# In a filler's slot the weights are split one chunk ahead of the filler's own, not two

## The chip, the cores and the metric

The kernel runs on one core of one Trainium2 chip. The metric is the device time of one execution in microseconds; the median of three runs of the kernel before is 2589.95 us (2587.48 to 2590.49). TensorE (PE) multiplies matrices into PSUM, VectorE (DVE) and ScalarE (ACT) do the elementwise work, and SyncE (SP) issues the transfers of the weights.

## The reference, cut to what matters

Two transformer stacks of two layers each run one after the other on a sequence of 256 tokens with 1024 features, all in float32:

```python
for l in range(DEPTH):                                  # first_block, DEPTH = 2
    h = rms_norm(x, norm_mix[l])
    x = x + (even_mixer if l % 2 == 0 else odd_mixer)(h, ...)   # projections, two kinds of attention, w_out
    x = x + memory_cross_attention(rms_norm(x, norm_cross[l]), rms_norm(mem, norm_mem[l]), ...)
    x = x + conv_ffn(rms_norm(x, norm_ffn[l]), ...)
for l in range(DEPTH):                                  # second_block
    x = x + HALF_STEP * swiglu(rms_norm_2(x, ffn1_norm[l]), ...)
    x = x + hybrid_mixer(rms_norm_2(x, mix_norm[l]), ...)       # fox, sparse and stick-breaking attention, gates
    x = x + memory_cross_attention_2(rms_norm_2(x, ca_norm[l]), rms_norm_2(mem, mem_norm[l]), ...)
    x = x + HALF_STEP * swiglu(rms_norm_2(x, ffn2_norm[l]), ...)
return rms_norm_2(x, final_norm)
```

Every `@` with a weight matrix is a linear layer. There are 8 mixers and cross attentions, and 6 feed-forward layers.

## The kernel before, in words

**Weights.** A weight matrix is cut into *chunks* of at most 128 x 2048 float32 (1 MB), numbered through the whole program in the order of use. Each chunk takes four steps. SP loads it into one of 3 slots `raw` (L639). ACT rounds it to `whi` (L1140), in one of 3 sets. DVE subtracts, `wlo = raw - whi` (L1503). PE multiplies with it, three products for each block: hi by lo, lo by hi, hi by hi (L727, L728, L730). ACT and DVE together *split* a chunk. ACT may not overwrite a set until PE has finished with the chunk three before (the `release` of the chunk). SP may not reload a slot until DVE has split the chunk three before (L635).

**Units.** A *unit* is one bank of PSUM: all products of (mostly) 256 output columns, 48 matmuls with a full chunk, 24 in an output projection, where two units share a chunk. Two banks alternate, so a unit waits until the unit two before has been *evacuated*, by ACT or by DVE, to SBUF.

**Stages.** The program is a list of stages, and PE, ACT and DVE each walk through it with a loop of their own. A `linear` stage works on its own units. For unit `un`, ACT and DVE first call `split_upto(un["chunk"] + 2)` and then evacuate. `heads`, `attention` (softmax, mlstm, difference, stick) and `index` stages compute attention, where PE would often wait, so units of the *next* linear layers are put between as *fillers*. A stage has a table `fill={slot: (emit_end, evac_end)}`: at that slot PE emits the units below `emit_end`, ACT and DVE split ahead and then evacuate the units below `evac_end`. The slot `"pre"` comes right behind the barrier at a stage's start (PE does it before its barrier), slots 0, 1, ... are turns of the attention loop or places in `heads`. A filler table advances by one unit a slot nearly everywhere.

**Where it is.** `split_upto` of ACT stands at L1124 to L1140, of DVE at L1489 to L1503, `fill` of ACT at L1160 and of DVE at L1545. In an attention loop on DVE the order of a turn is `fill`, then the softmax work of the units; on ACT `fill`, then the exponentials. In a `linear` stage whose output is a residual, DVE adds unit i to x (L1532), ACT then prepares two tiles of the next layer's input (L1186, L1189: `norm_pair`), and the next layer's first products (L757) start from those.

Filled stages in the order of time: the even mixer (heads, softmax, mlstm, heads, then a linear), the odd mixer (heads, softmax, heads, difference, heads, then a linear), four cross attentions (two with a heads stage, each ending in a linear of two chunks and four units), and two hybrid mixers (heads, index, three attentions, then the linear over three branches, whose chunks have 1536 and 768 columns in turn).

Of the kernel before, what the change touches and what calls it, by code (L numbers as in the profile page):

```python
# [159 lines left out]
def build(nc, io):  # L160
    ctx = ExitStack()
    with ctx:
# [104 lines left out]
        stages, chunks, units_of = [], [], []  # L267
# [836 lines left out]
        def _(eng):  # L1104
# [10 lines left out]
            def enter(i, st):  # L1115
                if i and not st["join"]:
                    eng.drain().then_inc(S["act_stage"], 1)
                    eng.wait_ge(S["pe_stage"], st["bar"])
                    eng.wait_ge(S["dve_stage"], st["bar"])
                    fill(st, "pre")  # L1120
# [3 lines left out]
            def split_upto(c):  # L1124

                while rounded[0] <= min(c, len(chunks) - 1):
                    i = rounded[0]
                    rounded[0] += 1
                    ch = chunks[i]
                    eng.wait_ge(loaded[i % SLOTS], ch["loaded"])  # L1130
                    if ch["mem"] is not None:
                        eng.wait_ge(S["lin_ready"], ch["last"] + 1)
                        eng.activation(X[ch["mem"]][0][:, :, :], raw[i % SLOTS][:, :].rearrange("p (k c) -> p k c", c=SEQ), ACT.Copy)\
                           .then_inc(S["weights_hi"], 1)
                        continue
                    s = ch["set"]
                    if s >= SETS:
                        name, value = chunks[set_chunks[s - SETS]]["release"]
                        eng.wait_ge(S[name], value)
                    eng.activation(whi[s % SETS][:, 0:ch["n"]], raw[i % SLOTS][:, 0:ch["n"]], ACT.Copy).then_inc(S["weights_hi"], 1)  # L1140
# [3 lines left out]
            def evac_upto(end):  # L1144

                while moved[0] < end:
                    u = moved[0]
                    un = units_of[u]
                    moved[0] += 1
                    if un["post"] != "plain":  # L1150
                        continue
                    eng.wait_ge(S["lin_ready"], u + 1)
                    if "dsts" in un:
                        (a, b, dst, _), = un["dsts"]
                        src = lin_bank[u % 2][:, :].rearrange("p (t c) -> p t c", t=QT)[:, :, a:b]
                    else:
                        dst, src = un["dst"], lin_bank[u % 2][:, 0:un["n"] * SEQ].rearrange("p (n c) -> p n c", c=SEQ)
                    eng.activation(dst, src, ACT.Copy).then_inc(S["lin_moved"], 1)

            def fill(st, slot):  # L1160

                if slot in st["fill"]:
                    emit_end, evac_end = st["fill"][slot]
                    split_upto(units_of[emit_end - 1]["chunk"] + 2)
                    evac_upto(evac_end)

            gated = [0]
# [118 lines left out]
            def heads(st):  # L1286
                if st["d"]:
                    norms_of_heads(st)
                    fill(st, 0)
                    fill(st, 1)  # L1290
                if st["gates"]:
                    gate_logs(st["gates"])
                for i, g in enumerate(st["groups"] if st["rope"] else ()):
                    eng.wait_ge(S["qk_roped"], st["r0"] + i + 1)
                    eng.activation(g["x"], banks[(3, 7)[i % 2]][:, 0:g["n"] * SEQ].rearrange("p (n c) -> p n c", c=SEQ), ACT.Copy).then_inc(S["qk_rot_used"], 1)
                    if i == 1 and not st["d"]:
                        fill(st, 0)

                if st["gates"]:
                    gate_rows(st["gates"])  # L1300
# [167 lines left out]
        def _(eng):  # L1468
# [9 lines left out]
            def enter(i, st):  # L1478
                if i and not st["join"]:
                    eng.drain().then_inc(S["dve_stage"], 1)  # L1480
                    eng.wait_ge(S["pe_stage"], st["bar"])
                    eng.wait_ge(S["act_stage"], st["bar"])
                    fill(st, "pre")
                if i == more_consts_at:
                    eng.wait_ge(S["more_consts_loaded"], 16)
# [3 lines left out]
            def split_upto(c):  # L1489

                while subtracted[0] <= min(c, len(chunks) - 1):
                    i = subtracted[0]
                    subtracted[0] += 1
                    ch = chunks[i]
                    n, full = ch["n"], raw[i % SLOTS]
                    eng.wait_ge(S["weights_hi"], i + 1)
                    if ch["mem"] is not None:
                        hi, lo = X[ch["mem"]]
                        eng.tensor_tensor(lo[:, :, :], full[:, :].rearrange("p (k c) -> p k c", c=SEQ), hi[:, :, :].bitcast(F32), ALU.subtract)\
                           .then_inc(S["weights_split"], 1)  # L1500
                        continue
                    s = ch["set"] % SETS
                    eng.tensor_tensor(wlo[s][:, 0:n], full[:, 0:n], whi[s][:, 0:n].bitcast(F32), ALU.subtract).then_inc(S["weights_split"], 1)  # L1503
# [3 lines left out]
            def evac_upto(end):  # L1507
                while evacuated[0] < end:
                    evacuated[0] += 1
                    evac(evacuated[0] - 1)  # L1510
# [34 lines left out]
            def fill(st, slot):  # L1545

                if slot in st["fill"]:
                    emit_end, evac_end = st["fill"][slot]
                    split_upto(units_of[emit_end - 1]["chunk"] + 2)
                    evac_upto(evac_end)  # L1550

            def norm_lo(nm, p):
# [145 lines left out]
            def heads(st):  # L1698
# [3 lines left out]
                if st["d"]:  # L1702
                    R = st["rows"]
                    eng.wait_ge(S["qk_rs"], st["n"] + 1)
                    newton(rstd[0:R, 0, 0:SEQ], rstd2[0:R, 0, 0:SEQ], post_bank[0][0:R, 0:SEQ], st["d"] * EPS, 0.5, S["qk_rows"], C(st["scale"])[0:R, :])
                    fill(st, 0)
                    for i, g in enumerate(gs):
                        eng.wait_ge(S["qk_spread"], g0 + i + 1)
                        norms = banks[i % 4][:, 0:g["n"] * SEQ].rearrange("p (n c) -> p n c", c=SEQ)
                        eng.scalar_tensor_tensor(out=g["x"], in0=g["x"], scalar=cols[:, g["gain"]:g["gain"] + 1], in1=norms,  # L1710
                                                 op0=ALU.mult, op1=ALU.mult).then_inc(S["qk_normed"], 1)
                    fill(st, 1)
# [311 lines left out]
```

## Time and profile before

| | |
|---|---|
| median of three runs | 2589.95 us |
| the profiled execution: its own time | 2590.67 us |
| its span | 2588.8 us |
| PE busy | 2394.8 us (93%) |
| DVE busy | 1603.0 us (62%) |
| ACT busy | 1096.6 us (42%) |
| chain of waits, by engine | PE 77%, DVE 11%, ACT 6% |
| granted TensorE clock, mean | 0.952 |
| a 1 MB load of weights, median from issue to landing | 5.1 us |

The span is what the trace covers; 1.9 us of the execution lie outside it. Shares of busy time are averages over the whole program; in the feed-forward layers PE never stops, in the filled stages it waits here and there, and only there can the order of the splits matter.

### The profile page before, as it was taken

The page shows a single profiled execution, that of the slowest core. Times are in us where ns is not written, and L with a number is a line of the kernel's source. Part 1 is how long each engine was busy: PE and PEld are TensorE (multiplying, and loading weights), DVE is VectorE, ACT ScalarE, POOL GpSimd, SP SyncE. Part 2 cuts the span into 40 slices and gives each one's busy share as a digit, 9 for nine tenths or more (in the row PEclk, how much of TensorE's full clock was granted, in tenths as well). Part 3 has the DMA queues.
Part 4 walks back from the last instruction along what each step waited for, and adds up shares of the span by engine and source line. Part 5 has one row for each costly group of instructions (what it writes and reads, how often), then busy time and mean ns, then how long its engine had stood idle before and what let it go on. Part 6 is the DMA issues. An engine that isn't in the chain of part 4 may idle for free.

```text
span 2588.8 us, 41000 instructions
## 1 busy us (share of the span) xinstructions
PE 2394.8 (93%) x17744; PEld 2239.1 (86%) x17744; DVE 1603.0 (62%) x2326; ACT 1096.6 (42%) x1329; POOL 34.8 (1%) x60
## 2 busy tenths in 40 slices
PE   6989999998799999999998799999999988889997
PEld 5868899986689999999967688999999967688997
DVE  4565587755457786656557646666666446655654
ACT  4435454533444444335334345334334324445332
POOL 1300000000000000000000000000000000000000
PEclk8889999998799999999989899999999989899999
DMA  8523245441134555555521344555556522244552
GB/s 256 173 70 132 96 165 194 164 146 59 56 129 167 187 172 179 186 176 153 180 78 54 113 163 136 176 177 182 177 179 179 172 66 77 68 151 145 175 185 82
DMA packets 318901, 373.79 MB, mean 144 GB/s; under 512 B 23647, under 2 KB 289651, under 8 KB 317571
## 3 DMA queue, kind: packets, MB, share of 16 engines
q1 hardware_dynamic: 313715, 353.32, 41.7%
q0 software_dynamic: 3424, 11.50, 1.5%
q10 hardware_dynamic: 1584, 6.36, 0.7%
q8 instruction: 140, 2.29, 0.4%
q14 instruction: 38, 0.31, 0.0%
HBM read 361.97 MB, written 9.18 MB: 143 GB/s over the span
## 4 chain that ended last, share of the span: by engine, by line
PE 77%; DVE 11%; ACT 6%; issue 2%; PEld 2%; DMA 1%; DVEq 0%; PEldq 0%; ACTq 0%
PE bank L727 20%; PE bank L730 20%; PE bank L728 20%; DVE wlo L1503 3%; ACT whi L1140 3%; PE bank L757 2%; PE bank L758 2%; PE bank L737 2%; PE bank L968 2%; PE bank L1017 2%; PE bank L761 2%; PE bank L897 1%; PE bank L1004 1%; ACT x_hi L1186 1%; DVE xT L1532 1%
## 5 line engine op out<-in xcount | busy, mean ns | idle before, releaser
L727 PE MATMUL bank<-x_hi,wlo 128*128 128x256 f32 (+1 forms) x4432 | 1143.9, 290 | 24.3 <-DVE wlo L1503 8.3
L728 PE MATMUL bank<-x_lo,whi 128*128 128x256 f32 (+1 forms) x4432 | 1131.4, 287 | 0.0
L1503 DVE TENSOR_TENSOR wlo<-raw,whi 128x2048 fp32r<-128x2048 f32 (+2 forms) x344 | 762.0, 2224 | 324.4 <-ACT whi L1140 324.2
L1140 ACT ACTIVATE whi<-raw 128x2048 fp32r<-128x2048 f32 (+2 forms) x344 | 638.9, 1860 | 719.4 <-PE bank L730 651.5
L727 PEld LDWEIGHTS bank<-x_hi,wlo 128*128 128x128 f32 (+1 forms) x4432 | 869.5, 196 | 51.5 <-issue 31.5
L728 PEld LDWEIGHTS bank<-x_lo,whi 128*128 128x128 f32 (+1 forms) x4432 | 870.2, 196 | 0.0
L730 PE MATMUL bank<-x_hi,whi 128*128 128x256 f32 x4432 | 710.9, 286 | 0.0
L730 PEld LDWEIGHTS bank<-x_hi,whi 128*128 128x128 f32 x4432 | 615.7, 195 | 4.6 <-issue 0.7
L757 PE MATMUL bank<-x_hi,wlo 128*128 128x256 f32 x544 | 154.8, 315 | 46.5 <-DVE xT L1532 19.8
L757 PEld LDWEIGHTS bank<-x_hi,wlo 128*128 128x128 f32 x544 | 111.3, 205 | 52.2 <-issue 32.0
L758 PE MATMUL bank<-x_lo,whi 128*128 128x256 f32 x544 | 144.1, 295 | 0.0
L1938 DVE TENSOR_TENSOR wk<-bank,norm_scale 128x512 f32<-128x512 f32 x132 | 91.1, 690 | 83.5 <-PE bank L730 77.4
L758 PEld LDWEIGHTS bank<-x_lo,whi 128*128 128x128 f32 x544 | 111.5, 205 | 1.2
L1976 DVE CAST x_hi<-wk 128x512 fp32r<-128x512 f32 x66 | 28.2, 427 | 131.9 <-PE bank L730 130.9
L1954 DVE SCALAR_TENSOR_TENSOR wk<-wk,cols 128x255 f32<-128x255 f32 x176 | 73.5, 480 | 48.0 <-ACT wk L1434 47.3
L727 PE MATMUL bank<-whi,x_lo 128*128 128x256 f32 (+2 forms) x400 | 99.7, 286 | 1.1 <-issue 0.8
L728 PE MATMUL bank<-wlo,x_hi 128*128 128x256 f32 (+2 forms) x400 | 98.5, 283 | 0.0
L1186 ACT ACTIVATE x_hi<-xT,con,cols 128x256 fp32r<-128x256 f32 x112 | 60.8, 590 | 84.7 <-DVE xT L1532 69.9
L1434 ACT ACTIVATE wk<-wk,cols 128x256 f32<-128x256 f32 x88 | 45.7, 590 | 98.1 <-DVE wk L1938 98.1
L1017 PE MATMUL bank<-wk,vt 128*64 128x256 f32 (+2 forms) x288 | 72.9, 392 | 11.4 <-ACT wk L1389 9.8
L727 PEld LDWEIGHTS bank<-whi,x_lo 128*128 128x128 f32 x400 | 77.7, 194 | 4.3 <-issue 3.8
L968 PE MATMUL bank<-ft 64*128 64x128 f32 (+2 forms) x216 | 62.8, 431 | 19.1 <-DVEq L1480 17.1
(225 smaller groups left out, 1986.9 us busy)
## 6 DMA issues: line engine op xcount, KB each, us to landing
raw<-in_ffn_w_gu SPq DMA_DIRECT2D x88, 1024.0 KB, 5.1
raw<-in_ffn_w_down SPq DMA_DIRECT2D x66, 1024.0 KB, 5.2
raw<-in_ffn_w_up SPq DMA_DIRECT2D x44, 1024.0 KB, 5.1
raw<-in_w_in SPq DMA_DIRECT2D x42, 1024.0 KB, 5.2
raw<-in_ca_w_kv SPq DMA_DIRECT2D x16, 1024.0 KB, 5.1
raw<-in_od_w_in SPq DMA_DIRECT2D x12, 1024.0 KB, 5.1
raw<-in_ev_w_in SPq DMA_DIRECT2D x10, 1024.0 KB, 5.3
raw<-in_w_in SPq DMA_DIRECT2D x20, 512.0 KB, 5.2
```

The lines of the kernel that those rows point to most:

```text
L727: eng.matmul(out, a[1], b[0], start=first and i == 0, stop=False, skip_group_check=True)
L728: eng.matmul(out, a[0], b[1], start=False, stop=False, skip_group_check=True)
L730: m = eng.matmul(out, a[0], b[0], start=False, stop=last and i == len(operands) - 1, skip_group_check=True)
L757: eng.matmul(bank[:, o], a[1], b[0], start=i == 0 and k == 0, stop=False, skip_group_check=True)
L758: eng.matmul(bank[:, o], a[0], b[1], start=False, stop=False, skip_group_check=True)
L968: m = eng.matmul(o, un["q"][:, t * P:(t + 1) * P], un["k"][:, 0:n], start=True, stop=row is None)
L1017: m = eng.matmul(ob[i % len(ob)][un["pb"]:un["pb"] + un["d"], q0:SEQ], un["v"][:, k, :], probsT_flat[i % 2][:, at:at + SEQ - q0], start=k ...
L1140: eng.activation(whi[s % SETS][:, 0:ch["n"]], raw[i % SLOTS][:, 0:ch["n"]], ACT.Copy).then_inc(S["weights_hi"], 1)
L1186: eng.activation(X[nm["buf"]][0][:, k, :], xT[:, k, :], ACT.Identity, scale=cols[:, nm["gain"] + k:nm["gain"] + k + 1], bias=C("zero")).th ...
L1503: eng.tensor_tensor(wlo[s][:, 0:n], full[:, 0:n], whi[s][:, 0:n].bitcast(F32), ALU.subtract).then_inc(S["weights_split"], 1)
L1938: return eng.tensor_tensor(wk[:, half, :].rearrange("p (n c) -> p n c", c=SEQ), bank[:, :].rearrange("p (n c) -> p n c", c=SEQ), norms, AL ...
L1954: m = eng.scalar_tensor_tensor(out=o, in0=wk[:, half, i * SEQ:(i + 1) * SEQ][:, src], scalar=cols[:, w:w + 1], in1=o, op0=ALU.mult, op1=AL ...
```

## The change

In a filler's slot ACT and DVE split up to one chunk ahead of the last unit emitted there, where they split up to two ahead before. `linear` and `ffn` stages still split two ahead.

```diff
@@ fill, ScalarE (L1160) and, the same line, VectorE (L1545)
                 if slot in st["fill"]:
                     emit_end, evac_end = st["fill"][slot]
-                    split_upto(units_of[emit_end - 1]["chunk"] + 2)
+                    split_upto(units_of[emit_end - 1]["chunk"] + 1)
                     evac_upto(evac_end)
```

All splits are still done, each once and in the same sequence; what moves is where they stand among the other instructions. On ScalarE in the even mixer's mlstm stage (L1357 and L1360 are its exponentials; the numbers name the sets and slots):

```order
-L1140 ACTIVATE whi1<-raw1 128x2048 [waits weights_loaded1,lin_ready,dve_stage,pe_stage]
+L1140 ACTIVATE whi0<-raw0 128x2048 [waits weights_loaded0,lin_ready,dve_stage,pe_stage]
 L1357 ACTIVATE wk<-wk,stat 128x256 [waits att_max]
 L1357 ACTIVATE wk<-wk,stat 128x256 x3
 L1360 ACTIVATE stat<-stat 128x4
-L1140 ACTIVATE whi2<-raw2 128x2048 [waits lin_ready,weights_loaded2]
+L1140 ACTIVATE whi1<-raw1 128x2048 [waits lin_ready,weights_loaded1]
 L1357 ACTIVATE wk<-wk,stat 128x256 [waits att_max]
 L1357 ACTIVATE wk<-wk,stat 128x256 x3
```

The place has a split before and after, but of the chunk before the former one, so `lin_ready` is waited for at an earlier value.

On VectorE at the end of the first cross attention (L1858 and L1860 are the last attention output, L1532 the residual of the linear stage's units):

```order
 L1858 CAST x0_hi<-bank7 128x256 [waits att_o]
 L1860 TENSOR_TENSOR x0_lo<-bank7,x0_hi 128x256 [waits dve_step]
-L1503 TENSOR_TENSOR wlo0<-raw1,whi0 128x2048 [waits weights_hi,act_stage,pe_stage]
+L1503 TENSOR_TENSOR wlo2<-raw0,whi2 128x2048 [waits weights_hi,act_stage,pe_stage]
+L1503 TENSOR_TENSOR wlo0<-raw1,whi0 128x2048 [waits weights_hi]
 L1532 TENSOR_TENSOR xT<-bank4,xT 128x512 [waits lin_ready]
 L1532 TENSOR_TENSOR xT<-bank5,xT 128x512 [waits lin_ready]
```

The linear stage behind the filled ones now opens with two splits where it had one; ScalarE's order moves in the same way. The split that is missing is the one of the first `"pre"` slot of each run of filled stages.

On VectorE in the first hybrid mixer's stick stage (three pieces in order of time: its first slot, its second, and the start of the linear stage behind it, whose first residual-like step is L1538):

```order
-L1503 TENSOR_TENSOR wlo2<-raw1,whi2 128x1536
+L1503 TENSOR_TENSOR wlo1<-raw0,whi1 128x2048
 L1528 SCALAR_TENSOR_TENSOR gt<-bank5,norm_scale 128x512
 L1777 SCALAR_TENSOR_TENSOR ft<-bank0,ft 128x384
...
-L1503 TENSOR_TENSOR wlo0<-raw2,whi0 128x768
+L1503 TENSOR_TENSOR wlo2<-raw1,whi2 128x1536
 L1528 SCALAR_TENSOR_TENSOR gt<-bank4,norm_scale 128x512
...
+L1503 TENSOR_TENSOR wlo0<-raw2,whi0 128x768
 L1503 TENSOR_TENSOR wlo1<-raw0,whi1 128x1536
 L1538 SCALAR_TENSOR_TENSOR ft<-gt,bank4 128x512
```

Here the chunks have unequal sizes, so the slots get larger splits than before. PE, SP and POOL keep their order word for word.

## Rows read from the trace of the kernel before

**Rows 1.** The page's chain that ended last, shares of the span:
```profile
PE 77%; DVE 11%; ACT 6%; issue 2%; PEld 2%; DMA 1%; DVEq 0%; PEldq 0%; ACTq 0%
```
**Rows 2.** The page's groups: line, operation, count, busy us, mean ns, idle before:
```profile
L1503 DVE TENSOR_TENSOR wlo<-raw,whi 128x2048 fp32r<-128x2048 f32 (+2 forms) x344 | 762.0, 2224 | 324.4 <-ACT whi L1140 324.2
L1140 ACT ACTIVATE whi<-raw 128x2048 fp32r<-128x2048 f32 (+2 forms) x344 | 638.9, 1860 | 719.4 <-PE bank L730 651.5
```
**Rows 3.** Timeline, ScalarE, mlstm: start us, length us, instruction, idle before and releaser:
```profile
157.99 0.19 ACT L1360 ACTIVATE stat<-stat 128x4 f32<-128x4 f32 x1
161.29 1.91 ACT L1140 ACTIVATE whi<-raw 128x2048 fp32r<-128x2048 f32 x1 [3.12 <-PE bank L730]
```
**Rows 4.** Timeline, VectorE, the same slot of the mlstm stage:
```profile
163.23 2.29 DVE L1503 TENSOR_TENSOR wlo<-raw,whi 128x2048 fp32r<-128x2048 f32 x1 [6.89 <-ACT whi L1140]
```
**Rows 5.** Timeline, TensorE, behind the filler of that slot:
```profile
169.73 0.80 PE L955 MATMUL bank<-ft 128*128 128x256 f32 x1 [3.54 <-DVE wk L1846]
```
**Rows 6.** Timeline, ScalarE, the linear stage that ends the first cross attention:
```profile
286.94 1.91 ACT L1140 ACTIVATE whi<-raw 128x2048 fp32r<-128x2048 f32 x1 [2.23 <-DVEq L1480]
291.91 1.09 ACT L1186 ACTIVATE x_hi<-xT,con,cols 128x256 fp32r<-128x256 f32 x2 [3.06 <-DVE xT L1532]
...
293.72 1.10 ACT L1186 ACTIVATE x_hi<-xT,con,cols 128x256 fp32r<-128x256 f32 x2 [0.19 <-DVE xT L1532]
...
295.24 1.90 ACT L1140 ACTIVATE whi<-raw 128x2048 fp32r<-128x2048 f32 x1
```
**Rows 7.** Timeline, VectorE, the same linear stage:
```profile
288.98 2.29 DVE L1503 TENSOR_TENSOR wlo<-raw,whi 128x2048 fp32r<-128x2048 f32 x1 [2.17 <-ACT whi L1140]
291.19 0.68 DVE L1532 TENSOR_TENSOR xT<-bank,xT 128x512 f32<-128x512 f32 x1
292.99 0.69 DVE L1532 TENSOR_TENSOR xT<-bank,xT 128x512 f32<-128x512 f32 x1 [1.11 <-PE bank L730]
...
297.18 2.29 DVE L1503 TENSOR_TENSOR wlo<-raw,whi 128x2048 fp32r<-128x2048 f32 x1 [2.71 <-ACT whi L1140]
299.39 0.68 DVE L1532 TENSOR_TENSOR xT<-bank,xT 128x512 f32<-128x512 f32 x1
```
**Rows 8.** Timeline, TensorE, the first product of the feed-forward layer behind it:
```profile
300.22 0.35 PE L757 MATMUL bank<-x_hi,wlo 128*128 128x256 f32 x1 [1.51 <-DVE xT L1532]
```
**Rows 9.** Timeline, VectorE, the even mixer's linear stage:
```profile
210.97 2.29 DVE L1503 TENSOR_TENSOR wlo<-raw,whi 128x2048 fp32r<-128x2048 f32 x1 [0.94 <-ACT whi L1140]
215.56 0.69 DVE L1532 TENSOR_TENSOR xT<-bank,xT 128x512 f32<-128x512 f32 x1 [2.30 <-PE bank L761]
```
**Rows 10.** Timeline, ScalarE, first slot of the first stick stage:
```profile
1409.98 1.49 ACT L1140 ACTIVATE whi<-raw 128x1536 fp32r<-128x1536 f32 x1
```
**Rows 11.** Timeline, VectorE, first and second slot of that stick stage:
```profile
1411.60 1.76 DVE L1503 TENSOR_TENSOR wlo<-raw,whi 128x1536 fp32r<-128x1536 f32 x1 [3.04 <-ACT whi L1140]
...
1421.49 0.95 DVE L1503 TENSOR_TENSOR wlo<-raw,whi 128x768 fp32r<-128x768 f32 x1
```
**Rows 12.** Timeline, TensorE, the scores of that stage's third head:
```profile
1417.30 0.92 PE L976 MATMUL bank<-ft 64*128 64x128 f32 x4 [0.87 <-DVE wk L1790]
```
**Rows 13.** Timeline, VectorE, the first hybrid mixer's linear over three branches:
```profile
1445.88 1.76 DVE L1503 TENSOR_TENSOR wlo<-raw,whi 128x1536 fp32r<-128x1536 f32 x1 [5.11 <-ACT whi L1140]
1447.67 0.69 DVE L1538 SCALAR_TENSOR_TENSOR ft<-gt,bank 128x512 f32<-128x512 f32 x1
```
**Rows 14.** Timeline, TensorE, the third unit of that linear stage:
```profile
1448.51 0.35 PE L727 MATMUL bank<-x_hi,wlo 64*128 64x256 f32 x1 [2.29 <-DVE ft L1538]
```
**Rows 15.** Timeline, ScalarE, behind the "pre" split of the first cross attention:
```profile
254.56 2.17 ACT L1307 ACTIVATE wk<-ft 128x512 f32<-128x512 f32 x4
```
**Rows 16.** Timeline, TensorE, the sums over those squares, behind the "pre" filler:
```profile
258.03 2.33 PE L884 MATMUL bank<-wk,con 128*8 128x256 f32 x10
```
**Rows 17.** Windows: us, busy of PE, PEld, DVE, ACT, POOL, then clock, DMA:
```profile
1448.80:1455.60 6.80, 6.80 (x27) 5.77 (x26) 3.50 (x6) 1.48 (x1) 0.00 (x0) 0.50 0.54 154
...
300.00:307.00 7.00, 6.78 (x50) 6.60 (x51) 5.16 (x9) 6.21 (x8) 0.00 (x0) 1.00 0.48 152
```

More of the change, by code:

```diff
@@ L1548, in fill @@
                     emit_end, evac_end = st["fill"][slot]
-                    split_upto(units_of[emit_end - 1]["chunk"] + 2)
+                    split_upto(units_of[emit_end - 1]["chunk"] + 1)
                     evac_upto(evac_end)
```

## The prediction

> **What bounds the kernel now.** I read the chain of waits first. It lies on PE for 77% of the span, on DVE for 11% and on ACT for 6% [rows 1]. The feed-forward layers are PE's alone and keep their order; DVE and ACT are on the chain in the mixers and cross attentions, and those are the stages that the change touches. Then the groups: 344 splits of 1.86 us on ACT and 2.22 us on DVE, in which DVE mostly waits for ACT and ACT mostly for PE to give a set free [rows 2]. The reader should not add this up: most of it is feed-forward, where it costs nothing. So I went through the timeline, one filled stage after another, with three questions: does PE wait here, what ends the wait, and does a split stand ahead of that.
>
> **The change as a whole.** No split is added or removed. A run of filled stages loses the split of its first "pre" slot (8 places: the first heads stage of each mixer and of two cross attentions, the attention of the other two) and its closing linear stage gets one more at its start (8 places). Between them every slot keeps one split, of the chunk before. That has two effects: ACT waits for an earlier release, and where chunks are unequal the slot's length changes.
>
> **The 8 opening splits, removed: 0.** In the first cross attention ACT, behind the split, squares the heads' inputs until 256.7 [rows 15], and PE takes up the squares at 258.03, with no idle time before, because its own filler ends only then [rows 16]. The cover is the "pre" filler, which ends 1.3 us later than the squares; taking 1.91 us away from ACT only widens that. Where I looked at the other openings, PE ran through in the same way. I take 0. The bound above is 0, the bound below 8 times 1.91 us off.
>
> **The release in the mlstm stage: 3.1 us saved.** ACT finishes its exponentials at 158.18 and then sits until 161.29, because the split in the second slot needs the set of a chunk on which PE is still busy with the filler of the slot before [rows 3]. DVE waits 6.89 us for it, splits from 163.23 [rows 4], and only then scales the probabilities for which PE waits 3.54 us [rows 5]. After the change the same place splits a chunk whose set has long been free. ACT starts at 158.15 or so, DVE at 160.1, ends at 162.3, behind the filler's end at 161.2 that its evacuation needs. Everything behind follows 3.1 us earlier, as DVE and ACT alternate on the chain until the stage ends. Late next is PE, whose next filler ends at 169.73 - 3.54 = 166.2, against probabilities at 169.7 - 3.1 = 166.6: there is hardly more to be had. Bounds: nothing saved, and 3.5 us, PE's wait. Elsewhere such waits for a release are under a filler of PE and give nothing.
>
> **The closing linear stages of the four cross attentions: 2.0 us lost each, 8.1 in all.** Now ACT splits once [rows 6], DVE behind it from 288.98, and adds unit 0 right behind that split, at 291.19, without waiting for PE [rows 7]. With two splits ACT does the second from 288.85, beside DVE's first. DVE does its two back to back, starts 2.21 us apart as between these rows, so unit 0 is added at 288.98 + 2 x 2.21 = 293.40. Unit 1, ready on PE since about 292.9, follows at once. ACT prepares the next layer's tiles 0.72 us behind unit 0's addition (291.91 - 291.19), so from 294.12; the second pair 1.62 us later without idle time (293.72 - 291.91 - 0.19), from 295.74; its next split 1.52 us after (295.24 - 293.72), at 297.26 instead of 295.24. Behind this split stand DVE's split and the addition of unit 2 [rows 7], for which the feed-forward's first product waits [rows 8]. That is 2.0 us later at the start of the feed-forward layer, and nothing behind gives it back. The timeline has the same rows at 760, 1565 and 2361 us. Bounds: 0, if the wait of 1.51 us and the others took it up, and 4.2 us, both halves of a split end to end.
>
> **The closing linear stages of the even and odd mixer: 0.** DVE splits at 210.97 and next has to add a unit that PE has ready only at 215.56 [rows 9]. A second split ends at 210.97 + 2.21 + 2.29 = 215.47, just in time; the odd mixer's linear stage has the same shape. The cover is PE's pair of units. If it fails, 0.1 us or so.
>
> **The hybrid mixers: 1.8 us lost each, 3.5 in all.** The stick stage's first slot now holds a split of 2048 columns instead of 1536. On ACT that is 1.91 - 1.49 = 0.42 us more [rows 10], on DVE 2.29 - 1.76 = 0.53 [rows 11], and both stand one behind the other on the way to the scores of the third head, for which PE waits on DVE [rows 12]. So 0.95 us; a filler stands behind those scores and the next head behind the filler, so it stays. The second slot grows from 768 to 1536 columns, 1.76 - 0.95 = 0.8 us on DVE [rows 11]; a filler of PE lies beside it, and I take 0, between 0 and 0.8. In the linear stage behind, ACT does a 768 split ahead of the 1536 one, about 0.8 us, DVE's 0.95 us of it lies beside ACT's second, and the first merge moves from 1447.67 to 1448.45 [rows 13]; PE waits for just that merge [rows 14]. So 0.8. Bounds for a whole mixer: 0, and 3.5 us, every added piece of ACT and DVE end to end.
>
> **Transfers: 0.** A slot is reloaded when its chunk is split, so reloads move by one slot in the filled stages. The latest is the second chunk of the feed-forward layer: its reload can now start only when the first of the two closing splits ends, at 291.3, and it is needed behind the feed-forward's first product, after 302. A megabyte takes 5.1 us from issue to landing (the page's DMA part), so another one ahead of it fits too.
>
> **Sum.** -3.1 + 8.1 + 1.9 + 1.6 = 8.5 us. The profiled execution took 2590.67 us, so 2599.2; it stands 0.72 us above the median, which gives 2598.4 us as the median after. The bounds taken all together run from 3.5 us faster to 4 x 4.2 + 2 x 3.5 = 24 us slower, without the openings. Below 0.2%, 5.2 us, a measurement of this kernel can't tell a change from none.
>
> **Rivals.**
>
> 1. *PE's clock falls on top.* In the cross attentions' closing stages PE's waits grow: one of about 1.1 us arises before unit 2 (unit 0 added by 294.1, PE free from 292.9), and the 1.51 us become about 2.1. In the hybrid's linear a wait of 2.29 us [rows 14] is followed by 6.8 us at a granted clock of 0.50, 1.2 GHz [rows 17], while behind the 1.51 us it stays at 1.00, 2.4 GHz [rows 17]. One such stretch costs 3.4 us of PE's work. If two of the four get one, the sum is 15.3 and the time 2605. Against it: the added waits are shorter than 2.29 us. The Trainium skill, "TensorE: Matmul & The Clock Gate", section "What's actually happening", says that the default is the slow clock and that activity releases it, so more waiting can only hurt; the rows agree in direction, and by that rule this rival would be the forecast.
>
> 2. *The cross attentions hide the second split.* Then -3.1 + 3.5 = 0.4 and the time is 2590.4: no change. For it: PE waits 1.51 us before the feed-forward layer anyway. Against it: that wait ends by the very addition that moves.
>
> 3. *Faster: the opening splits were on the path.* If the squares behind the "pre" split, and not the filler, held PE's sums, each of the 8 openings would give 1.91 us, 15.3 in all, and 8.5 - 15.3 = -6.8 puts the time at 2583. It decides from the point where a "pre" filler ends before ACT's squares do. Against it are the 1.3 us of room [rows 15, 16].
>
> 4. *The change doesn't do what it says*, as PE would at some slot stand before a chunk that is not split yet. Each filler's chunk is still split in the slot before its own, and DVE passes that slot before PE gets to the next. Where it did happen, it would cost up to 4.2 us a time; I count it with rival 1.
>
> **How the numbers follow.** The forecast has 0.57, with a range of its own of 2595 to 2602. Rival 1 (with 4) has 0.15, rival 2 with its partial forms, in which the terms shrink below 5.2 us, 0.21, rival 3 0.07. So slower 0.72, the same 0.21, faster 0.07. The range of 2592 to 2606 takes in rival 1 and half of rival 2's and leaves out rival 3.
>
> **What would show it.** Right: ACT's L1140 in the mlstm stage starts at about 158.1 with no wait for PE, and PE's wait of 3.54 us is gone; the four cross attentions' linear stages show two L1503 in a row and the first L1532 2.2 us later, the feed-forward's first product 2.0 us later; the mixers' additions at 215.56 don't move against the product's start; the third stick head's scores start 0.95 us later; openings on PE look as before. Wrong: PE's L757 behind the cross attentions starts as far from the stage's start as now; a heads stage gets shorter; PE waits for L1503 inside a filled stage; or the stretches at half clock add up to more than the terms.

## The result, and the profile after

| | before | changed |
|---|---|---|
| median, four runs each | 2588.72 us | 2603.6 us |
| the profiled execution: time, span | 2590.67, 2588.8 us | 2604.47, 2602.6 us |
| chain of waits | PE 77%, DVE 11%, ACT 6% | PE 76%, DVE 12%, ACT 7% |
| granted TensorE clock, mean | 0.952 | 0.952 |

The changed kernel is slower: the ratio is 1.0062, 95% interval 1.0049 to 1.0075, 13 to 19 us. The forecast of 2598.4 us had the sign and its range (2592 to 2606) holds the time, but it gives only a bit more than half of the loss.

TensorE runs the same instructions in the same order in both kernels, so I followed the start of each of them through both traces. Where the difference of the starts jumps, time is lost or won. I call this comparison the ledger. These are its jumps from before to after, in us:

| stretch | forecast | trace |
|---|---|---|
| start to the mlstm stage (not the change's, see below) | 0 | -3.5 |
| mlstm stage | -3.1 | -3.2 |
| closing stages of the four cross attentions, to the feed-forward's first product | 4 x 2.0 = 8.1 | 1.90, 1.91, 2.18, 1.91 = 7.9 |
| the feed-forward layers' first part behind them | 0 | 1.46, 1.58, 1.59, 1.59 = 6.2 |
| first hybrid mixer, second | 1.75 each | 3.4, 3.1 |
| the rest: other openings, the other mixers' closings | 0 | about 0 |

The sum is 13.8 us but for rounding, the difference of the spans. First the mlstm stage, which answers to [rows 3 to 5]: timeline of the changed kernel, start us, length us, instruction, idle before and releaser.

```profile
154.47 0.19 ACT L1360 ACTIVATE stat<-stat 128x4 f32<-128x4 f32 x1
154.56 1.90 ACT L1140 ACTIVATE whi<-raw 128x2048 fp32r<-128x2048 f32 x1
156.49 2.29 DVE L1503 TENSOR_TENSOR wlo<-raw,whi 128x2048 fp32r<-128x2048 f32 x1 [3.67 <-ACT whi L1140]
162.98 1.13 PE L955 MATMUL bank<-ft 128*128 128x256 f32 x4 [1.84 <-DVE wk L1846]
```

ScalarE's split starts right behind the exponentials, its wait of 3.12 us is gone, and VectorE's wait has fallen from 6.89 to 3.67 us. TensorE still waits 1.84 us, where it waited 3.54. From ScalarE's last exponential (L1360) to the product L955 it is 8.51 us here, 11.74 before [rows 3, 5].

Not all of that is the change's. The release that ScalarE waited for comes from TensorE's filler, and in the trace of before this filler ran at half clock. The kernel `e10_hybrid_heads_slot` below has these splits as before, but its filler ran at full clock. First its ScalarE, then the windows over the filler, before and in that kernel:

```profile
154.90 0.19 ACT L1360 ACTIVATE stat<-stat 128x4 f32<-128x4 f32 x1
155.19 1.91 ACT L1140 ACTIVATE whi<-raw 128x2048 fp32r<-128x2048 f32 x1
```

```profile
152.00:158.60 6.60, 6.60 (x30) 6.07 (x29) 4.17 (x12) 1.80 (x5) 0.00 (x0) 0.50 0.46 151
```

```profile
149.00:155.50 6.50, 6.50 (x52) 6.37 (x52) 4.15 (x12) 2.12 (x6) 0.00 (x0) 1.00 0.49 155
```

Its split starts 0.10 us behind the exponentials without the change, and from L1360 to L955 it is 8.72 us. So the change is worth 3.2 us here when the filler runs at half clock, and 0.2 when it does not. Of the five traces with these splits as before, three have the whole wait (3.11 or 3.12 us), one has 1.60 and one none.

The closing stage of the first cross attention answers to [rows 6 to 8]. It starts at 280.20 here, at 286.94 before.

```profile
280.20 3.72 ACT L1140 ACTIVATE whi<-raw 128x2048 fp32r<-128x2048 f32 x2 [2.23 <-DVEq L1480]
282.25 4.49 DVE L1503 TENSOR_TENSOR wlo<-raw,whi 128x2048 fp32r<-128x2048 f32 x2 [2.18 <-ACT whi L1140]
286.66 1.28 DVE L1532 TENSOR_TENSOR xT<-bank,xT 128x512 f32<-128x512 f32 x2
287.49 0.36 PE L727 MATMUL bank<-x_hi,wlo 128*128 128x256 f32 x1 [1.29 <-DVE xT L1532]
290.41 1.90 ACT L1140 ACTIVATE whi<-raw 128x2048 fp32r<-128x2048 f32 x1
292.34 2.29 DVE L1503 TENSOR_TENSOR wlo<-raw,whi 128x2048 fp32r<-128x2048 f32 x1 [3.34 <-ACT whi L1140]
294.55 0.68 DVE L1532 TENSOR_TENSOR xT<-bank,xT 128x512 f32<-128x512 f32 x1
295.38 0.36 PE L757 MATMUL bank<-x_hi,wlo 128*128 128x256 f32 x1 [1.90 <-DVE xT L1532]
```

Two splits in a row stand ahead of the first addition, which comes 6.46 us behind the stage's start instead of 4.25. TensorE now waits twice, 1.29 us before unit 2 and 1.90 before the feed-forward layer. From the stage's start to the layer's first product it is 15.16 us (295.38 - 280.22), against 13.26 (300.22 - 286.96).

Then the clock. Here are windows of 3.4 us at the feed-forward layers behind the second, third and fourth cross attention: columns as in [rows 17], the seventh is the granted clock. Before:

```profile
773.20:776.60 3.40, 3.39 (x25) 3.29 (x26) 2.87 (x7) 3.40 (x7) 0.00 (x0) 1.00 0.86 279
1578.70:1582.10 3.40, 3.39 (x25) 3.29 (x26) 2.87 (x7) 3.40 (x7) 0.00 (x0) 1.00 0.87 283
2374.20:2377.60 3.40, 3.40 (x27) 3.29 (x27) 2.79 (x7) 3.40 (x7) 0.00 (x0) 1.00 0.92 304
```

After:

```profile
773.10:776.50 3.40, 3.40 (x14) 3.04 (x14) 1.68 (x4) 3.40 (x5) 0.00 (x0) 0.50 1.08 387
1585.40:1588.80 3.40, 3.40 (x15) 3.04 (x14) 1.95 (x5) 3.40 (x5) 0.00 (x0) 0.51 0.83 284
2387.60:2391.00 3.40, 3.40 (x15) 3.04 (x14) 1.60 (x4) 3.40 (x5) 0.00 (x0) 0.50 0.70 245
```

TensorE is busy all through both, and gets through 25 to 27 instructions in one and 14 or 15 in the other. These are three new stretches at 1.2 GHz, 1.6 us each in the ledger. The mean clock doesn't show them, because other stretches went.

The 1.46 us at the first feed-forward layer are something else. TensorE does wait inside the first two feed-forward layers, for VectorE's splits. Its wait 43 us behind the first closing stage, before and after:

```profile
343.19 0.39 PE L727 MATMUL bank<-x_hi,wlo 128*128 128x256 f32 x1 [1.22 <-DVE wlo L1503]
338.33 0.39 PE L727 MATMUL bank<-x_hi,wlo 128*128 128x256 f32 x1 [2.70 <-DVE wlo L1503]
```

Before, a stretch of 3.4 us at half clock lay ahead of this wait and was taken up by it; after, the stretch lies behind it and costs its 1.5 us.

The first stick stage and the linear stage behind it [rows 10 to 14], after:

```profile
1412.11 2.29 DVE L1503 TENSOR_TENSOR wlo<-raw,whi 128x2048 fp32r<-128x2048 f32 x1 [3.46 <-ACT whi L1140]
1418.34 1.22 PE L976 MATMUL bank<-ft 64*128 64x128 f32 x3 [1.83 <-DVE wk L1790]
...
1449.49 0.96 DVE L1503 TENSOR_TENSOR wlo<-raw,whi 128x768 fp32r<-128x768 f32 x1 [4.46 <-ACT whi L1140]
1450.77 1.76 DVE L1503 TENSOR_TENSOR wlo<-raw,whi 128x1536 fp32r<-128x1536 f32 x1 [0.32 <-ACT whi L1140]
1452.56 0.69 DVE L1538 SCALAR_TENSOR_TENSOR ft<-gt,bank 128x512 f32<-128x512 f32 x1
```

TensorE's wait for the third head's scores grew from 0.87 to 1.83 us, the 0.95 of the forecast. What the forecast didn't have follows at once, in windows at the same place before and after:

```profile
1417.20:1424.00 6.80, 6.70 (x52) 6.32 (x52) 5.68 (x11) 3.49 (x7) 0.00 (x0) 1.00 0.04 15
```

```profile
1418.20:1425.00 6.80, 6.66 (x28) 6.01 (x29) 6.61 (x11) 3.35 (x6) 0.00 (x0) 0.50 0.05 16
```

### The profile page after: what moved, and what is told of

Its sections match the earlier page's. It is cut to its first block, busy times and chain, and to the rows that moved or that the text cites. A ratio compares the mean times of both kernels' runs of the same rounds, so it can differ in the third digit from the quotient of the medians.

```text
span 2602.6 us, 41000 instructions
## 1 busy us (share of the span) xinstructions
PE 2401.4 (92%) x17744; PEld 2244.2 (86%) x17744; DVE 1603.4 (62%) x2326; ACT 1096.0 (42%) x1329; POOL 34.9 (1%) x60
## 3 DMA queue, kind: packets, MB, share of 16 engines
q8 instruction: 140, 2.29, 0.4%
## 4 chain that ended last, share of the span: by engine, by line
PE 76%; DVE 12%; ACT 7%; issue 2%; PEld 2%; DMA 0%; DVEq 0%; ACTq 0%; PEldq 0%
PE bank L727 20%; PE bank L730 19%; PE bank L728 19%; DVE wlo L1503 4%; ACT whi L1140 3%; PE bank L757 3%; PE bank L758 2%; PE bank L737 2%; PE bank L968 2%; PE bank L1017 2%; PE bank L761 2%; PE bank L897 1%; ACT x_hi L1186 1%; PE bank L1004 1%; DVE wk L1756 1%
```

## The experiments

Theory: the chain terms of the forecast, and on top of them rival 1, new stretches at half clock behind waits that have grown. Rivals: the chain alone; and an accident of one execution. Times are ratios to the kernel before, run beside it on the same chip, with their 95% intervals; 0.001 is 2.6 us. The changed kernel was timed beside runs of before of its own, so a distance to it is the difference of two ratios, good to 4 or 5 us.

**One part of the change at a time.** `ahead=1` was given to some stages, the rest kept 2.

```diff
-                    split_upto(units_of[emit_end - 1]["chunk"] + 2)
+                    split_upto(units_of[emit_end - 1]["chunk"] + st.get("ahead", 2))
```

*The four cross attentions.* 

> One chunk ahead only in the filled stages of the four cross attentions, so that each closing linear stage starts with two splits. Theory of the chain: 2.0 us each, 8 us slower. Theory of the chain and the clock (rival 1 of the prediction): the same 8 us and about 1.6 us more at the start of each feed-forward layer, from stretches of 3.4 us at half clock that follow the longer waits: 14 us slower, with the stretches at 773, 1585 and 2388 us as in the changed kernel. If the stretches come from something else in the changed kernel (the hybrids, the mlstm stage, the accident of one execution), they are missing here and the time is 8 us above.

Measured: 1.0059 (1.0045 to 1.0073), 15 us. Even the lower end, 11.6 us, lies above the 8 us of the chain alone. The ledger has the same four closing terms (1.89, 1.91, 2.18, 1.91) and 1.59 at the second and third feed-forward layer. The fourth shows nothing (0.01), so the stretch isn't certain even where the waits are. This trace is of the slowest of the five executions (2606.18 us, median 2601.62), and 3.7 us of its ledger lie behind 2080 us at places that the edit doesn't touch. The two stretches and the chain come to 11.1 us, so the time can't tell one stretch more or less.

*The two hybrid mixers.* 

> One chunk ahead only in the filled stages of the two hybrid mixers. The forecast has 0.95 + 0.8 us for each, 3.5 us slower. If the longer waits of the stick stage also bring half-clock stretches, as in the trace of the changed kernel (a stretch of 6.8 us at 1418 that before lacks), it is 3.1 to 3.4 us each, 6 to 7 us slower. In the trace the first merge of the linear stage over three branches comes 0.8 us later against that stage's start.

Measured: 1.0032 (1.0014 to 1.0051), 4 to 13 us. The interval is wide because of one execution of ten at 2615.91 us; the medians lie 6.4 us apart. The ledger has 6.0 us in all and repeats the changed kernel's jump in the first stick stage (3.9 us in both), with a stretch of 6.8 us at 1418. The four closing stages are unchanged (0.00 each). But the first feed-forward layer is 1.50 us later here, though nothing before it was changed: of the 1.46 us in the table above, nothing can be put down to the change. That leaves the three stretches, 4.8 us.

*The mlstm stage.* 

> One chunk ahead only in the mlstm stage, two everywhere else. If the release wait is worth what the forecast says, 3.1 us faster than before; by the two traces, which lose 1.7 us from the stage's second slot to the heads behind it, 1.7 us faster. If that loss was the clock's, and not the split's, no change. In its trace ScalarE's split of the second slot starts right behind the exponentials without a wait for PE, and TensorE's wait of 3.54 us there is down to about 1.8. At the start of the feed-forward layers there is no new stretch at half clock, and the closing stages of the cross attentions are as before.

Measured: 0.9993 (0.9984 to 1.0002), no difference that can be told; 4.1 us faster is still inside. The ledger has -3.9 us in the stage, and +2.2 in the heads stage behind it. There the pre slot, which splits two ahead, now has two splits to do:

```profile
191.29 3.71 ACT L1140 ACTIVATE whi<-raw 128x2048 fp32r<-128x2048 f32 x2 [0.25 <-DVEq L1480]
193.33 4.49 DVE L1503 TENSOR_TENSOR wlo<-raw,whi 128x2048 fp32r<-128x2048 f32 x2 [2.34 <-ACT whi L1140]
195.45 1.89 PE L884 MATMUL bank<-wk,con 128*4 128x256 f32 x8 [1.56 <-ACT wk L1307]
198.57 0.36 PE L727 MATMUL bank<-x_hi,wlo 128*128 128x256 f32 x1 [1.24 <-DVE xT L1532]
```

TensorE waits 1.56 us for squares that stand behind the second split. That is rival 3's mechanism, and it takes two splits in an opening to bring it out. In the changed kernel the heads stage has one, and pays nothing.

**Where the split stands against the addition.** The changed kernel with, in VectorE's `linear`, the addition ahead of the split, at first in all stages with a residual:

```diff
-                    split_upto(un["chunk"] + 2)
+                    late = un["post"] in ("residual",)
+                    split_upto(un["chunk"] + (0 if late else 2))
...
                     evac_upto(un["u"] + 1)
+                    split_upto(un["chunk"] + 2)
```

> The changed kernel, and in the linear stages whose output is a residual VectorE adds the unit first and does the split of two chunks ahead behind it. If the loss of the cross attentions is the place of the split ahead of the addition, TensorE no longer waits 1.3 us before unit 2 nor 1.9 us before the feed-forward's first product: 3.2 us less in each of four, and 1.57 us less in each of the even and odd mixers, 16 us off the changed kernel, 1 us faster than before; with the half-clock stretches gone as well 22 us off, 7 us faster than before. If ScalarE's order or the transfers hold these stages, nothing changes against the changed kernel: 15 us slower than before.

Measured: 1.0031 (1.0020 to 1.0042), 8 us below the changed kernel, not 16 or 22. The closing stages gained 3.1 to 3.4 us each, as the theory has it, but the even and odd mixers lost 2.9 and 5.7 us. Two things go wrong there. The edit puts off the split of the next chunk too, which there is not done yet, and TensorE waits 1.55 us for it; this is made up by the next layer's first product. Then TensorE waits about 3.1 us for the addition of unit 3, which now stands behind a split, and this stays; in the odd mixer a stretch at half clock behind it adds 2.7 us. The second try keeps the next chunk's split ahead (`+ 1` instead of `+ 0`) and leaves the mixers alone:

> The changed kernel; in the closing linear stages of the cross attentions VectorE does only the split of the next chunk ahead of an addition, and that of two chunks ahead behind it. The mixers' closing stages are left alone, which the earlier run of this kind did not do. If the loss of the cross attentions is the place of that split, TensorE's waits of 1.28 and 1.90 us go, and with them the half-clock stretches: 3.2 + 1.6 us in each of four, 19 us off the changed kernel, 4 us faster than before. If the stretches stay, 13 us off, 2 us slower than before. If ScalarE or a transfer holds the stage, no change against the changed kernel, 15 us slower than before.

Measured: 1.0013 (1.0004 to 1.0022), 12.7 us off the changed kernel. The ledger gives 3.6, 3.6, 3.8 and 3.6 us in the closing stages and 0.4, 2.0, 0.3 and 0.6 behind them; no stretch at half clock is left there, but TensorE waits 0.84 us for the split that now comes last. So the place of the split ahead of the addition is shown as the cause of the cross attentions' loss. The time alone sits at "stretches stay", 13 us.

**The clock by itself.** Dummy matmuls of constants fill TensorE's two waits of each closing stage and change nothing else.

```diff
+                    keep = nm is None and parts is None and len(units) == 4
+                    for _ in range(8 if keep and i == 2 else 0):
+                        eng.matmul(banks[2][:, 0:P], C("add128"), C("ident"), start=True, stop=True)
                     if i >= 2 or (nm is None and parts is None):
                         unit(u)
+                    for _ in range(13 if keep and i == 3 else 0):
+                        eng.matmul(banks[2][:, 0:P], C("add128"), C("ident"), start=True, stop=True)
```

> The changed kernel with dummy matmuls on TensorE (of constants, into a bank that nothing reads) in its two waits of each cross attention's closing linear stage: 8 ahead of unit 2 and 13 behind unit 3, about 0.13 us each. They leave the chain alone and only keep TensorE busy. If the waits bring the half-clock stretch at the start of the feed-forward layers, the stretches go and the time is 4 to 6 us below the changed kernel, 9 to 11 us above before. If the stretches have another cause, they stay, and the time is that of the changed kernel, 15 us above before, or more where the dummies are longer than the waits.

Measured: 1.0068 (1.0056 to 1.0081), no gain. The dummies took 1.95 and 3.07 us, longer than the waits, which cost 1.0 us a stage. All three stretches went, and with them 1.6 us each; the dummies eat 3.9 us of that, and stretches elsewhere take the rest. With 5 and 8 of them:

> The changed kernel with dummy matmuls in TensorE's two waits of each closing stage as before, but 5 and 8 of them instead of 8 and 13, since one takes 0.24 us and the earlier ones were longer than the waits by 0.7 and 1.2 us. If the half-clock stretches at the start of the feed-forward layers come from these waits, and nothing else is changed by the dummies, 4.8 to 6.2 us faster than the changed kernel, 9 to 10 us slower than before. If the stretches come of their own, 15 us slower than before.

The timeline of TensorE in this kernel, where each dummy shows as two records, and the first of the windows above:

```profile
760.79 1.28 PE L872 MATMUL bank<-con 128*128 128x128 f32 x10
762.24 0.36 PE L727 MATMUL bank<-x_hi,wlo 128*128 128x256 f32 x1 [0.17 <-DVE xT L1537]
768.06 1.95 PE L876 MATMUL bank<-con 128*128 128x128 f32 x16
```

```profile
770.10:773.50 3.40, 3.38 (x25) 3.29 (x26) 2.87 (x7) 3.40 (x7) 0.00 (x0) 1.00 0.86 287
```

In the trace this is clear: the four closing terms are unchanged (0.00, 0.00, 0.01, 0.00), the three stretches are gone, and the layers' starts are 1.6 us faster each. One trace could be an accident, but every kernel's trace has the four places. Three kernels have both waits and leave them unfilled: the changed one, the one with the cross attentions alone and the one with two ahead in the pre slots, below. They have a stretch that starts within 1.5 us of the layer's first product in 8 of 12 places (3, 2 and 3 of 4). The other eleven kernels, the two with dummies among them, have it in none of 44. That TensorE's idle time in the two waits brings the stretches is thereby shown in the traces.

The times don't bear it out: 1.0058 (1.0045 to 1.0070), 15 us above before where 9 to 10 were expected. The profiled execution (2599.12 us) was the fastest of five; the others reach 2604.45. Even the profiled one loses 1.6 us near 2067 us and 1.7 behind 2500, in half-clock stretches that are longer or new there though nothing was changed. Where TensorE's clock falls differs from one execution to the next, and whether the others lost the whole gain again in such places stays open.

**The openings.** The changed kernel with two ahead in the pre slots:

```diff
-                    split_upto(units_of[emit_end - 1]["chunk"] + 1)
+                    split_upto(units_of[emit_end - 1]["chunk"] + (2 if slot == "pre" else 1))
```

> The changed kernel, except that the first slot of a stage (pre) splits two ahead as before; slots 0, 1, ... split one ahead. So the eight openings have their split back, in the cross attentions and wherever else the pre slot is followed by slots without a new chunk. If the openings cost nothing, the time is that of the changed kernel, 15 us above before. If the missing opening splits were worth something (rival 3), it is up to 15 us slower than the changed kernel; and if the openings' place is what the closing stages need, it would be faster than the changed kernel.

Measured: 0.9997 (0.9988 to 1.0005), none of the three: 17 us faster than the changed kernel. The closing stages are as slow as before (0.00 against the changed kernel), and the openings show nothing. The time comes from a place that the prediction doesn't look at, the rotations in the hybrid mixers' heads stage (L1725 and L1726 on VectorE, L909 and L910 on TensorE), -7.9 us in the first and -9.2 in the second against before; 1.5 of the latter are a shorter stretch at half clock ahead of it. With a split in the opening, slot 0 of that stage has none. The kernel before:

```profile
1290.20 1.90 ACT L1140 ACTIVATE whi<-raw 128x2048 fp32r<-128x2048 f32 x1
1292.14 2.29 DVE L1503 TENSOR_TENSOR wlo<-raw,whi 128x2048 fp32r<-128x2048 f32 x1 [11.51 <-ACT whi L1140]
1294.35 0.68 DVE L1528 SCALAR_TENSOR_TENSOR gt<-bank,norm_scale 128x512 f32<-128x512 f32 x1
1294.95 0.68 DVE L1725 TENSOR_TENSOR wk<-ft,con 128x512 f32<-128x512 f32 x1
1296.29 2.08 PE L909 MATMUL bank<-wk,con 128*128 128x512 f32 x2 [6.40 <-DVE wk L1726]
```

VectorE waits for ScalarE's split, does its own and an evacuation, and only then prepares the next rotation (L1725, L1726), for which TensorE waits 6.40 us; then it runs at half clock, with L909 at 2.08 us. This stood in the trace of before, and the change leaves it as it is, since it swaps one chunk for another in that slot. So I tried it alone, in the kernel before: `ahead=1` for that heads stage, with pre slots at 2, which moves this split to the next stage's start.

> Two chunks ahead as in before, but in slot 0 of the hybrid mixers' heads stage one ahead, which leaves that slot without a split (its chunk comes two at a time in the index stage's pre slot). The run with two ahead in the pre slots alone was 15 us faster than forecast, and its trace lost 7.9 and 9.2 us in just these two stages. If this one split is the cause, 16 us faster than before, with ScalarE's and VectorE's steps of the rotations 4.8 us earlier behind the third and the rest from half-clock stretches that go. If it was the accident of one execution, no change.

Measured: 0.9945 (0.9933 to 0.9958), 14 us faster than before. The same rotation:

```profile
1285.39 0.69 DVE L1725 TENSOR_TENSOR wk<-ft,con 128x512 f32<-128x512 f32 x1 [6.79 <-PE bank L910]
...
1286.74 1.13 PE L909 MATMUL bank<-wk,con 128*128 128x512 f32 x2 [0.53 <-DVE wk L1726]
```

VectorE now starts as soon as TensorE's last product is done, the wait is 0.53 us instead of 6.40, and the product takes 1.13.

**A better kernel.** First the addition ahead of the split in the kernel before, where the next chunk is always split already:

> The kernel before, two chunks ahead everywhere; only in linear stages whose output is a residual VectorE adds a unit before the split that stood ahead of it. Theory: in before, the split of two ahead stands between TensorE's unit 2 and its addition, and TensorE waits 1.5 us for that addition ahead of each of the four feed-forward layers and 1.57 us ahead of the first product of two cross attentions. Moved behind, these six waits go: 9 us faster than before. Rival: the chunk that is split later is the next one TensorE needs, so the wait only changes its name: no change. The clock could add to it either way, 1.6 us a stretch.

Measured: 0.9992 (0.9983 to 1.0002), no difference that can be told. The four closing stages gain 1.7 us each, about their wait. In the even and odd mixers the first product comes 1.8 us earlier, but the next layer's second unit uses the bank of unit 3, whose addition now stands behind the split:

```profile
222.34 2.29 DVE L1503 TENSOR_TENSOR wlo<-raw,whi 128x2048 fp32r<-128x2048 f32 x1 [1.96 <-ACT whi L1140]
225.34 0.69 DVE L1532 TENSOR_TENSOR xT<-bank,xT 128x512 f32<-128x512 f32 x1
226.17 0.35 PE L757 MATMUL bank<-x_hi,wlo 128*128 128x256 f32 x1 [2.69 <-DVE xT L1532]
```

The wait only moved, and with the clock behind it costs 4.0 us, more than the 1.8 won. Then the same with the merges of the hybrids and the mlstm stage added (`un["post"] in ("residual", "merge")`, `ahead=1` for mlstm):

> As the kernel of this call that adds first, and in addition one chunk ahead in the mlstm stage, and in the hybrids' linear over three branches VectorE merges a unit before its split. Theory: 9 us for the additions, 1.7 to 3.1 us for the mlstm stage, 2.3 us for each of two merges, and a half-clock stretch less behind each of those waits (up to 3.4 us each): 15 to 22 us faster than before. Rival: the merges and the mlstm stage are hidden elsewhere: 9 us faster.

Measured: 0.9948 (0.9937 to 0.9960), 13 us faster; a bit less than the theory's 15 to 22, as the mixers again lose 4.0 us each behind their gain of 1.0 and 1.7. Last, all that had paid, without the even and odd mixers' closings:

> The version to which the runs so far point: as before, with one ahead in the mlstm stage, slot 0 of the hybrids' heads stage without a split, and VectorE's addition or merge ahead of the split of two chunks ahead in the cross attentions' closing stages, the hybrids' linear over three branches and the hybrids' last linear (not in the even and odd mixers, where the trace showed a new wait of 2.7 us for unit 3's addition). If the parts add up, 13 us of the kernel that added and merged first, 16 us of the hybrids' heads, and 4 us from the mixers left alone: 33 us faster than before. If the waits of one part only move to another, 13 to 16 us faster.

Measured: 0.9887 (0.9869 to 0.9905), 29 us faster than the kernel before and 45 than the changed one. This rests on three executions, of 2556.04 to 2560.11 us, against a median of 2586.91; a fourth took 9313.22 us at a granted clock of 1.00, is not in the ratio, and has no trace that could explain it. The parts add up nearly (33 expected). Its first closing stage, beside [rows 6 to 8]:

```profile
287.22 0.68 DVE L1532 TENSOR_TENSOR xT<-bank,xT 128x512 f32<-128x512 f32 x1
...
290.07 0.69 DVE L1532 TENSOR_TENSOR xT<-bank,xT 128x512 f32<-128x512 f32 x1 [1.38 <-PE bank L730]
291.39 2.29 DVE L1503 TENSOR_TENSOR wlo<-raw,whi 128x2048 fp32r<-128x2048 f32 x1 [0.62 <-ACT whi L1140]
```

The addition of unit 2 at 290.07 waits for TensorE, not TensorE for it. Still open in this kernel are the 2.2 us of the double split behind the mlstm stage.

## Why the prediction was right, and where it was short

The sign was right, and so were most terms of the chain. That the range held the time is owed to rival 1: the range had been made to take it in, at a chance of 0.15, and it is what came.

**Cross attentions: right.** 8.1 us forecast, 7.9 us in the trace, and within 0.03 us of that in every kernel that left these stages so. Rival 2, that they hide the second split, is out. Adding first turned the loss around by 3.6 us a stage, so the mechanism is shown.

**The clock: the step that failed.** Rival 1 had a chance of 0.15, and I argued against it that the added waits "are shorter than 2.29 us". They are, one by one: 1.29 and 1.90 us. But three stretches of 3.4 us at half clock followed them, 1.6 us each, and one of 6.8 us in the first stick stage behind a wait of 1.83 us, 3.0 us. I compared the length of single waits, where the two waits stand some 6 us apart. The rule of the Trainium skill that I set beside it ("TensorE: Matmul & The Clock Gate", section "What's actually happening") says that the slow clock is the default and activity lifts it. The traces agree in direction: 0.50 behind the idle waits at 773.10 us, 1.00 behind the filled ones at 770.10. By that rule rival 1 would have been the forecast, and its time of 2605 is close to the 2603.6 measured. How far the clock explains the times and not only the traces is less sure: the time of the run with the cross attentions alone speaks for it, those with the filled waits don't.

**Mlstm stage: the number right, the worth of it in part luck.** -3.1 us forecast, -3.2 in the trace, -3.9 in the kernel with this part alone, which is beyond the bound of 3.5. The chain is as forecast, but the wait of 3.12 us was taken from a trace whose filler ran at half clock. With the filler at full clock the same splits as before have no such wait, and the change is worth 0.2 us. The forecast priced a stretch of the clock there without saying so. That TensorE's wait of 3.54 us would be gone was wrong: 1.84 us stay, since its filler, too, ended sooner at the full clock.

**Hybrid mixers: the chain right, the sum short.** 3.5 us forecast, 6.5 in the trace. The wait before the third head's scores grew by 0.96 us in both mixers against 0.95 forecast, and the third unit of the linear stage came 0.86 and 0.63 us later against 0.8. Stretches at half clock make the rest: 3.0 us behind the scores in the first and 1.5 back in its linear stage, where 6.8 us became 3.4, and 1.5 us in the second.

**Openings: right for one split, and for the changed kernel 0.** Rival 3's mechanism exists, but needs two splits in an opening, as the mlstm run showed.

**Transfers: 0, right.** In both traces the only wait of TensorE that ends at a transfer is the one for the input x at the start. **Rival 4** did not come up: inside a filled stage TensorE never stood before an unsplit chunk for more than 0.2 us.

**The start.** The ledger's -3.5 us ahead of the mlstm stage is not the change's. The seven kernels that keep the splits there as before have anything from -0.3 to -3.8 us at that point, by the first transfer's landing and by where the stretches at half clock fall. Without it the trace would show 17 us, where the times say 15.

**The feed-forward layers.** That TensorE never stops there, as said before the prediction, doesn't hold for the first two: it waits 1.82 and 2.72 us for splits at 801.75 and 816.20 us of the trace before. The change leaves these waits alone, but they decide what a stretch at half clock costs beside them.

## What to carry to other kernels

How far ahead a helper runs matters less than what stands behind it on its engine: a split of 1.9 us on ScalarE and 2.3 on VectorE cost 1.7 to 1.9 us ahead of an addition for which TensorE waited, and a wait of 6.40 us ahead of a rotation. Behind it it cost little, unless it then stood ahead of the next addition (4.0 us lost in each of two mixers). Ask this at every place where the helper stands, also where a change only swaps one piece of work for another; here that place was worth 14 us. Before a wait is priced, look at the clock under the work that ends it: the 3.12 us of the mlstm stage were there only at half clock. And when a wait grows, count the clock behind it, with all the waits that are near it.

## What the runs showed of the hardware

- Two waits of 1.29 (1.55 at the third place) and 1.90 us on TensorE, some 6 us apart, were followed by 3.4 us at a granted clock of 0.50 in 8 of 12 places in three kernels; with the same waits filled by matmuls of constants it stayed at 1.00 in 8 of 8, and with only a wait of 1.5 us or none in 36 of 36.
- The stretch isn't tied to the waits alone: in the run with the cross attentions alone the fourth layer had the waits and no loss (0.01 us).
- A stretch of 3.4 us at half clock costs nothing where TensorE waits soon behind it anyway: the wait at 343.19 us was 1.22 us with one ahead of it, and 2.70 without.
- The closing stages' chain terms repeat to 0.03 us from kernel to kernel, while stretches of the clock come and go between executions (that these set the spread of several us in the times is likely, not shown).
- A dummy float32 matmul of 128 x 128 by 128 columns took 0.24 us at the full clock (1.95 us for eight).
